# State-space products and head splits moved from GpSimd to VectorE, and small matmuls reordered, in a two-layer hybrid encoder

## The reference

```python
def mixer_ab(xn, w_in, w_out, ...):
    q, k, v, u = split(xn @ w_in)            # 1024 columns each
    o_a = dilated_attention(q, k, v, t5)     # 8 heads of 128
    y = (s5_direction(u, ..., reverse=False) + s5_direction(u, ..., reverse=True) + d_skip * u)
    y = gelu(y)
    o_b = y * sigmoid(y @ w_glu)
    return concat([o_a, o_b]) @ w_out
```

## Time and profile before

| what | us |
|---|---|
| median of 3 runs (2376.09 to 2386.47) | 2384.89 |
| the profiled execution | 2384.85 |
| its span (first to last instruction) | 2383.1 |
| busy PE, DVE, ACT, POOL | 2261.5, 1634.6, 1036.7, 285.2 |

### The profile page before, as it was taken

One profiled execution on the slowest core, in us unless ns is written; L12 is line 12 of the kernel. 1 busy time (PEld: TensorE's weight loads), 2 busy tenths in 40 slices (PEclk: granted clock), 3 DMA queues, 4 the chain that ended last, 5 costly groups with the idle time before them and its releaser, 6 DMA issues.

```text
span 2383.1 us, 40168 instructions
## 1 busy us (share of the span) xinstructions
PE 2261.5 (95%) x13779; PEld 1965.2 (82%) x13779; DVE 1634.6 (69%) x2617; ACT 1036.7 (44%) x1457; POOL 285.2 (12%) x201
## 2 busy tenths in 40 slices
PE   6887696999999999999999999999999999999997
PEld 5776576888888888888888888888888888888886
DVE  7999638767656656656658777766765765765765
ACT  6542124454444444444445444445444444444442
POOL 3560013230000000000131000022000000000023
PEclk9999798999999999999999999999999999999999
DMA  7533543556755755755755665655565566565663
GB/s 199 159 117 123 116 136 111 157 161 199 196 186 186 204 180 185 209 185 177 209 185 162 188 188 173 189 174 163 190 201 185 185 194 185 191 194 180 197 189 115
DMA packets 439240, 418.47 MB, mean 176 GB/s; under 512 B 49664, under 2 KB 434896, under 8 KB 438640
## 3 DMA queue, kind: packets, MB, share of 16 engines
q1 hardware_dynamic: 435952, 414.30, 57.6%
q10 hardware_dynamic: 3200, 3.03, 0.4%
HBM read 406.87 MB, written 10.39 MB: 175 GB/s over the span
## 4 chain that ended last, share of the span: by engine, by line
PE 84%; DVE 12%; ACT 1%; issue 1%; DMA 1%; POOL 0%; SPq 0%; DVEq 0%; ACTq 0%
PE psum L1505 53%; PE psum L1506 27%; DVE whl L916 5%; DVE ysum L916 3%; DVE wv L916 1%; PE psum L1691 1%; PE psum L1672 1%; PE psum L1669 1%; DVE wst L916 1%; DMA raw<-in_mlp_w 0%; ACT whl L599 0%; DVE tmpd L916 0%; DMA xin<-in_x 0%; PE psum L1711 0%; DVE ss_a L1237 0%
## 5 line engine op out<-in xcount | busy, mean ns | idle before, releaser
L916 DVE TENSOR_TENSOR whl<-raw,whl 128x1024 fp32r<-128x1024 f32 x744 | 964.7, 1309 | 503.3 <-ACT whl L599 501.4
L599 ACT ACTIVATE whl<-raw 128x1024 fp32r<-128x1024 f32 x744 | 788.2, 1061 | 854.7 <-PE psum L1506 740.1
L1505 PE MATMUL psum<-act,whl 128*128 128x512 f32 x3072 | 1096.5, 401 | 43.8 <-DVE whl L916 32.7
L1506 PE MATMUL psum<-act,whl 128*128 128x256 f32 x3072 | 863.1, 281 | 0.0
L1505 PEld LDWEIGHTS psum<-act,whl 128*128 128x128 f32 x3072 | 583.8, 190 | 187.7 <-DVE whl L916 33.3
L1505 PE MATMUL psum<-hid,whl 128*128 128x512 f32 x2048 | 717.3, 396 | 1.1 <-DVE whl L916 1.1
L1506 PEld LDWEIGHTS psum<-act,whl 128*128 128x128 f32 x3072 | 585.8, 191 | 0.1
L1506 PE MATMUL psum<-hid,whl 128*128 128x256 f32 x2048 | 571.3, 279 | 0.0
L1505 PEld LDWEIGHTS psum<-hid,whl 128*128 128x128 f32 x2048 | 384.4, 188 | 93.9 <-DVE whl L916 1.4
L1506 PEld LDWEIGHTS psum<-hid,whl 128*128 128x128 f32 x2048 | 385.7, 188 | 0.0
L610 ACT ACTIVATE half<-psum 128x256 f32<-128x256 f32 x376 | 123.8, 381 | 345.6 <-PE psum L1506 344.8
(11 more groups left out here) (195 smaller groups left out, 1529.4 us busy)
## 6 DMA issues: line engine op xcount, KB each, us to landing
raw<-in_mlp_w SPq DMA_DIRECT2D x512, 512.0 KB, 4.0
raw<-in_c_w_qkv SPq DMA_DIRECT2D x96, 512.0 KB, 4.6
raw<-in_ab_w_in SPq DMA_DIRECT2D x64, 512.0 KB, 4.1
raw<-in_ab_w_out SPq DMA_DIRECT2D x32, 512.0 KB, 4.3
raw<-in_c_w_out SPq DMA_DIRECT2D x32, 512.0 KB, 4.4
raw<-in_s_w_glu SPq DMA_DIRECT2D x8, 512.0 KB, 3.9
bias_c<-rpb_pad SPq DMA_DIRECT2D x64, 64.0 KB, 2.4
rpb_pad<-rpbw SPq DMA_DIRECT2D x4, 889.0 KB, 10.6
```

Of the source, the lines that this page charges most:

```text
L599: nc.scalar.activation(whl[:, s, :, 0, :], raw[:, s], ACT.Copy).then_inc(hi_done, 1)
L916: return nc.vector.tensor_tensor(dst, s0, s1, op)
L1505: pe.matmul(bank, *big, start=first, stop=False, skip_group_check=True)
L1506: last = pe.matmul(bank[:, 0:T], *little, start=False, stop=final, skip_group_check=True)
```

## The change

- **GpSimd to VectorE.** `in_weights(q, part)` makes both parts on VectorE, one quarter per block in blocks 1 to 4. `out_weights(k)` makes `fa` on VectorE: the four large operations one per sub in block 5, the eight small ones in the first three subs of block 6. `head_low` is VectorE's too. GpSimd keeps norms, masks of the second attention and small tables.
- **Ring and slots.** Transposes of quarter q stand at block q+2, the products one block later, so quarters 1 and 3 move. Scans start one sub later (25 slots for 26), `local_kernel` one block earlier.
- **Joined products.** In the first projection a pair becomes three matmuls of 256 columns into the same half bank (`joined=True`). ScalarE then copies the finished tile to its place (`take_tiles`), and VectorE's sums of blocks 0 to 15 are gone. ScalarE also takes x back (`take_x` before).
- **Mask and count.** The one-hot matrix gets a 33rd row with the logarithm of the count, or -1e30 at 0. `exps` now gives the sum (`accum_out`), VectorE only the reciprocal, and ScalarE scales (`scale_probs`).
- **Quadrants.** `chunk_outputs` puts both `mloc` products of a pair first and then steps through the quadrants.

```diff
-SCAN_SLOTS = [(j, s) for j in range(6, 13) for s in range(4)][2:]
+SCAN_SLOTS = [(j, s) for j in range(6, 13) for s in range(4)][3:]
...
@@ vector @@
+            def in_weights(q, part):
...
+                w, g0 = wst[:, q % 2, part], QG * q
+                tt(w, bcast_j(bt, 0, g0), bcast_c(aw, part, g0), ALU.mult).then_inc(w_mul, 1)
+                tt(tmpd[:], bcast_j(bt, 1, g0), bcast_c(aw, 1 - part, g0), ALU.mult).then_inc(w_mul, 1)
+                v.wait_ge(w_mul, 2 * (m + 1))
+                tt(w, w, tmpd[:], ALU.add if part else ALU.subtract).then_inc(w_done, 1)
+
+            def out_weights(k):
...
+                    made = tt(fa[:, 0], bcast_j(ct, 0, 0, NG), bcast_c(af, 0, 0, NG), ALU.mult)
+                if k == 1:
+                    v.wait_ge(ring_tr, RING["W", NQ - 1, 3] + 1)
+                    made = tt(fa[:, 1], bcast_j(ct, 1, 0, NG), bcast_c(af, 1, 0, NG), ALU.mult)
+                if k == 2:
+                    made = tt(fa[:, 0], fa[:, 0], fa[:, 1], ALU.add)
+                if k == 3:
+                    made = tt(fa[:, 1], bcast_j(ct, 0, 0, NG), bcast_c(af, 1, 0, NG), ALU.mult)
+                if k >= 4:
+                    g0 = QG * ((k - 4) // 2)
+                    here = fa[:, 1, g0:g0 + QG]
+                    if k % 2 == 0:
+                        made = tt(tmpf[:], bcast_j(ct, 1, g0), bcast_c(af, 0, g0), ALU.mult)
+                    else:
+                        made = tt(here, here, tmpf[:], ALU.subtract)
+                made.then_inc(fa_step, 1)
...
-                if j == 1 and s in (0, 2):
-                    in_weights_real(s // 2)
-                if j == 3 and s in (0, 2):
-                    in_weights_real(2 + s // 2)
+                if 1 <= j <= 4 and s in (0, 2):
+                    in_weights(j - 1, s // 2)
+                if j == 5:
+                    out_weights(s)
+                if j == 6 and s < 3:
+                    for k in ((4, 5, 6), (7, 8, 9), (10, 11))[s]:
+                        out_weights(k)
...
                 if g + 1 < HA:
-                    probs(g + 1, (g + 1) % 2, ss_a, cnt_a)
+                    inverse_sums(g + 1, (g + 1) % 2)
+                if g + 2 < HA:
+                    head_low(g + 2)
                 if g == 3:
                     for t in range(NT):
                         gelu_low(t)
@@ scalar @@
+                for n in range(2):
+                    src = psum[:, 2 * (j % 2) + n, 0:T]
...
+                    nc.scalar.activation(dst, src, ACT.Copy).then_inc(tiles_out, 1)
...
+            def scale_probs(h):
+                a.wait_ge(inv_done, h + 1)
+                for qt in range(2):
+                    nc.scalar.activation(ss_a[:, h % 2, qt], ss_a[:, h % 2, qt], ACT.Copy,
+                                         scale=stat[:, h % 2, 2, qt:qt + 1]).then_inc(prob_done, 1)
...
                 if g + 1 < HA:
-                    exps(g + 1, (g + 1) % 2, ss_a, False)
+                    exps(g + 1, (g + 1) % 2, ss_a, True)
@@ tensor @@
+                        if joined:
...
+                                parts = ((w, tile[:, 0, :]), (w, tile[:, 1, :]), little)
+                            for c, (w, m) in enumerate(parts):
+                                last = pe.matmul(bank[:, 0:T], w, m, start=(first and c == 0), stop=(final and c == 2),
+                                                 skip_group_check=True)
...
+                    for i in range(2):
+                        for g in range(2):
+                            pe.matmul(psum[NST * g:NST * (g + 1), fwd, NC * pp + 1:NC * (pp + 1)],
+                                      fa[0:NST, i, 2 * p + g].rearrange("p j c -> p (j c)"),
...
```

More of the change, by code:

```diff
@@ L540, in head_low @@
-            def head_low(h):
-                pool.wait_ge(head_hi, 2 * h + 2)
-                tt(qk_s[:, h % 3, :, 1], qk_a[:, :, h], qk_s[:, h % 3, :, 0].bitcast(F32), ALU.subtract) \
-                    .then_inc(head_split, 1)
-                tt(v_s[:, h % 3, 1].rearrange("p (k d) -> p k d", k=2), v_a[:, :, h * HD:(h + 1) * HD],
-                   v_s[:, h % 3, 0].rearrange("p (k d) -> p k d", k=2).bitcast(F32), ALU.subtract) \
-                    .then_inc(head_split, 1)
-            for h in range(HA):
-                head_low(h)
-                pool.wait_ge(mask_in, 32)
-                pool.wait_ge(bias_in[h % 2], 32 * (h // 2 + 1))
-                nc.gpsimd.tensor_tensor(bias_a[:, h % 2], bias_a[:, h % 2], neg_a[:], ALU.add).then_inc(bias_masked, 1)
@@ L853, in _ @@
                                      u[:, f].rearrange("p (j i) -> p j i", j=LC), ACT.Copy, scale=0.25).then_inc(ob_hi, 1)
-            loop_blocks(J_OUT0, 8)
+            high(0, J_OUT0, 0, 3)
+            for s in range(4):
+                for g in (2 * s, 2 * s + 1):
+                    a.wait_ge(x_tr, g + 1)
+                    nc.scalar.activation(x[:, 2 * g:2 * g + 2].rearrange("p k t -> p (k t)"), psum[:, 4 + g % 4, :],
+                                         ACT.Copy).then_inc(x_ready, 2)
+                if s < 3:
+                    high(0, J_OUT0, 1, s)
+            take_halves(0, J_OUT0, 0)
+            block_step(0, J_OUT0, 1)
+            loop_blocks(J_OUT0, 8, first=True)
             mlp(1, J_MLP0, 32)
@@ L1334, in _ @@
                     .then_inc(ob_ready, 1)
-            evac_out0 = residual(16)
-            low(0, J_OUT0, 0, 3)
-            for s in range(4):
-                take_x(2 * s)
-                take_x(2 * s + 1)
-                if s < 3:
-                    low(0, J_OUT0, 1, s)
-            evac_out0(0, J_OUT0, 0)
-            block_step(0, J_OUT0, 1, evac_out0)
-            loop_blocks(J_OUT0, 8, evac_out0, first=True)
+            loop_blocks(J_OUT0, 8, residual(16))
             def mlp(n, j0, gains, x0, h0, last=False):
@@ L1480, in norm, with sub_mm @@
                 pe.matmul(psum[:, 7, 0:T], ones[:], ssum[:], start=True, stop=True).then_inc(norm_mm, 1)
[L1482 removed]
+            def sub_mm(i, j0, jb, s, operand, ready, token_major=False, joined=False):
                 banks = 2 * ((j0 + jb) % 2)
@@ L1675, in chunk_outputs @@
                                       skip_group_check=True)
-                        for i in range(2):
-                            last = pe.matmul(psum[rows, bwd, NC * pp:NC * (pp + 1) - 1],
+                            last = pe.matmul(psum[NST * g:NST * (g + 1), bwd, NC * pp:NC * (pp + 1) - 1],
                                              fa[NST:P, i, 2 * p + g].rearrange("p j c -> p (j c)"),
@@ L1748, in v_sub @@
             def v_sub(k):
-                sub_mm(0, J_HEADS + k // 4, 0, k % 4, from_act, nothing, token_major=True)
+                sub_mm(0, J_HEADS + k // 4, 0, k % 4, from_act, nothing, token_major=True, joined=True)
             v_sub(0)
@@ L1883, in shape_constants @@
 def shape_constants():
-    rel = np.arange(T)[None, :] - np.arange(T)[:, None]
     branches = ((128, 1), (512, 4), (2048, 16))
-    cnt = sum(((rel % d == 0) & (np.abs(rel) <= w // 2)).astype(np.float32) for w, d in branches)
+    rel = np.arange(512) - 255
+    cnt = sum(((rel % d == 0) & (np.abs(rel) <= w // 2)).astype(np.float64) for w, d in branches)
+    reach = np.where(cnt > 0, np.log(np.maximum(cnt, 1)), NEG)
     c = np.arange(GRID_W)
```

266 lines of the change are left out of this document (105 added, 161 removed).

## The result

The changed kernel takes **2340.01 us** (median of 4 runs, 2338.89 to 2353.34), the kernel before beside it 2384.44 (4 runs, 2376.09 to 2386.47): ratio 0.983, 95% interval 0.981 to 0.986. The prediction, 2341, stands. The profiled execution took 2338.89, its span 2337.1 us against 2383.1 before, 46.0 less.

What follows compares the result with a forecast made beforehand. VectorE, slowed beside GpSimd and then full with scans, bounds up to 277.54 us, TensorE the rounds, then relays in the heads. From 2384.85, minus 24.0, minus 21.8, plus 1.8 gives 2341 us; range 2328 to 2364.

Steps and rivals of the forecast that it cites:

- TensorE bounds blocks 2 to 6: Before the first round: TensorE sets the pace from block 2 at 53.60 until sub (5, 0) is done at 102.9.
- VectorE then without a break: After sub (5, 0): VectorE bounds again, scans begin at 140, the first round at about 253.7.
- Stretch A: Everything up to the first round, 277.75 us before; forecast to give 24 us, bounds 16 and 30.
- Long rows are GpSimd's doing: Early VectorE work: its operations are slow where GpSimd works on long rows; one of 1.21 us takes about 3.
- rival 5: Early VectorE rows are long for another reason, such as DMA traffic, and stay; kernel slower, 2396 us; chance 3%.
- Column halves overlap: In the rounds, products of both column halves run side by side: a pair 0.70 us, a round 5.6.
- rival 1: In the rounds the column halves take turns: a pair 1.09 us, a round 8.7, total 2355; chance 15%.
- B: The stretch of rounds and subs, 277.75 to 335.30, 57.55 us before; forecast 35.7, so 21.8 us saved.
- The heads cost 1.8: Heads, after the rounds: moving low parts to VectorE keeps the relay; net cost 1.8 us, bounds -2 and +6.
- +3.2 for the detour: Heads, cycle 3: VectorE's GELU low parts stand behind `head_low(5)`, so `glu_sub` on TensorE waits 3.2 us more.
- +0.5 over the last cycles: Last cycles of the heads: reads of the accumulated sums add 0.5 us.
- C: The stretch of the heads, after the rounds; forecast to cost 1.8 us, bounds -2 and +6.

Runs made afterwards that it cites:

- pool_products: The changed kernel with the imaginary input weights and all products on `fa` back on GpSimd as before; 2359.35 us.
- unjoined: The changed kernel with the projection's products as before: two matmuls a tile, halves copied and summed; four executions took 2330.78, 2331.05, 2342.56 and 2355.12 us.
- after_again: The changed kernel itself executed once more, unedited, as a control on the same chip and in the same call; 2338.92 us.
- pool_noise: The changed kernel with twelve unneeded multiplications of 128x1024 elements on a scratch tile added on GpSimd; 2342.79 us.
- warm: The changed kernel with ninety unused matmuls of 256 columns added in TensorE's wait ahead of the first round; median 2335.88 us.
- heads_pool: The changed kernel with `head_low` back on GpSimd, all else as changed; 2339.11 us.
- quad_alone: The kernel before with only `chunk_outputs` issuing its products in the new order, both column halves side by side; 2363.44 us beside 2384.79.

## Why the prediction was right, step by step

- **TensorE bounds blocks 2 to 6.** Right. Sub (5, 0) was forecast to end at 102.9, and ends at 103.5; the low part behind it was forecast at 103.9, and starts at 104.86.
- **VectorE then without a break.** Right: scans at 141.00 (140 forecast), first round at 254.19 (253.7). Stretch A gives 23.6 us, 24 forecast. `pool_products` puts 19.0 of it on GpSimd's products and `unjoined` 3.3 on the tile sums, less what joining costs TensorE.
- **Long rows are GpSimd's doing** (against rival 5). Right and shown, by work that shares no data with VectorE's. What I put down as rows that "stretch" is a turn for each of GpSimd's instructions.
- **Column halves overlap** (against rival 1). Right and shown, in two kernels. A round takes 5.24 us and not 5.6: I had taken 0.70 for a pair, with 0.06 for dispatch that is hardly there (0.65). Subs 10.1 us (10.3), round 0 8.38 (8.6). B saves 23.3 and not 21.8. Part of that is the draw: `after_again` takes 34.1 us for B, `pool_noise` 35.4 with the same rounds, as the lower clock lasts longer behind round 0. The Trainium skill, page "TensorE: Matmul & The Clock Gate", section "Part 3: Packing small matmuls — row/col tiling", lets a weight load overlap only with another row group; by that B would have saved some 8 us. The trace does not agree: four starts within 0.02 us at 266.82, and 23.3 us. The same section's table of measured speed-ups does point this way: it has three column tiles 2.38 times faster.
- **The store at 7 us does not bound the rounds.** Right: they follow every 8.3 us.
- **The heads cost 1.8.** They cost -0.2. The terms up to `glu_sub` hold: -5.2 was forecast for moving the low parts off GpSimd (1.1 a cycle for three cycles, and 1.9 of stretched rows), and the experiments give -4.9 to -5.1; +3.2 for the detour, and they give 3.1 to 4.0, while TensorE's wait shrinks by 4.6; `glu_sub` is 1.1 later relative to the end of the rounds (0.7 forecast, with 0.9 a cycle for scalings and sums). The term that failed is the last one, "+0.5 over the last cycles". From the scores behind `glu_sub` to the output blocks the changed kernel takes 29.9 us, 1.3 less than before, and so do all its variants but `warm` (30.5) and `heads_pool`; `quad_alone`, whose heads are those of before, takes 30.7. I had priced only the accumulator's reads there. The move of the low parts is not what makes it shorter, as `heads_pool` does without it and takes 28.6; which of the other edits does was not tried. The rest is the draw: in `after_again` 1.5 us more pass between `glu_sub` and these scores, and C takes 93.6 us, 1.3 more than before.
- **The time behind the output blocks stays.** Off by 1.0 us, and no run shows why. It is 1955.2 to 1957.8 us in all profiled executions with one MLP stretch at each pace (last section), 1955.5 before and 1956.5 after.
- **Joined products cost 0.008 us a pair.** Right: 0.07 us a sub, 0.009 a pair. It is inside A's 23.6.

A gave 0.4 less than forecast, B 1.5 more and C 2.0 more, 3.1 us in all; that the total is within 1 us owes something to the 1.0 given back behind them, and to the median lying 1.1 above the profiled execution. Of the ten executions of the changed kernel seven took 2338.9 to 2341.1 us, two 2325 to 2326 and one 2353: the forecast names the most frequent time, and a single execution could have missed it by 14 us.

## What to carry to other kernels

An operation moved from GpSimd to VectorE costs VectorE its own length but frees up to one turn for every GpSimd instruction beside it (1.69 us at 128x1024); count the turns, not the rows. Where small products leave part of the array idle, put those of other rows and columns next to each other in the order before anything else. An operation that waits for a relay should not stand ahead of ready ones on its engine; one swap of that kind moved the output blocks by 2.3 us, a filler of ninety matmuls by 1.0 (3.6 and 2.3 beside the second execution of the changed kernel).

## What the hardware showed that was not expected

**TensorE has two paces at full granted clock.** Stretches of the changed kernel, then of the same kernel once more (`after_again`):

```profile
700.00:1000.00 300.00, 300.00 (x1700) 260.24 (x1699) 188.45 (x291) 127.18 (x159) 0.00 (x0) 1.00 0.64 192
2000.00:2300.00 300.00, 300.00 (x1733) 264.52 (x1731) 195.14 (x296) 129.63 (x162) 24.88 (x22) 1.00 0.61 189
```

```profile
700.00:1000.00 300.00, 300.00 (x1733) 264.49 (x1732) 191.31 (x295) 129.39 (x162) 0.00 (x0) 1.00 0.65 197
2000.00:2300.00 300.00, 300.00 (x1733) 264.54 (x1732) 191.09 (x287) 127.42 (x160) 29.91 (x27) 1.00 0.58 183
```

Identical code, TensorE never idle, clock 1.00 in all four rows, and 1700 matmuls in 300 us or 1733: a pair in 0.353 or 0.346 us. The kernel has two MLP stretches (some 500 to 1200 and 1600 to 2320 us), and a whole one keeps one pace, which makes 13 to 14 us over its length. That is nearly all of what parts the two executions, whose output blocks start within 1.3 us of each other and which end at 2337.1 and 2323.2. `unjoined` had the slower pace in both stretches (1700 and 1701) and 2353.3; before and the changed kernel have the same pair of paces (1701 and 1733, 1700 and 1733), so the pace has no part in their difference of 46.0 us. What chooses the pace stays open: it changes between executions of one kernel, and no run here tried to set it. It is also why four executions can't tell 5 us in this kernel, and a trace can.

**How long the lower clock lasts after a wait differs between executions of one kernel.** TensorE behind its wait of 8.21 us for `glu_sub`, the changed kernel (`glu_sub` starts at 343.74), then `after_again` (343.58):

```profile
346.75 0.28 PE L1721 MATMUL psum<-act,whl 128*128 128x256 f32 x1
...
350.69 0.87 PE L1668 MATMUL psum<-qk_s 128*128 128x256 f32 x6
```

```profile
349.82 0.28 PE L1721 MATMUL psum<-act,whl 128*128 128x256 f32 x1
...
352.01 0.88 PE L1668 MATMUL psum<-qk_s 128*128 128x256 f32 x6
```

The first row of each is the first of its kind at the full clock; until then such a row lasts 0.41 us. The lower clock (1.2 GHz) lasts 3.0 us in one execution and 6.2 in the other, the granted clock up to the scores is 0.79 and 0.64, and the way to them is 1.5 us longer. From the first round to the second pass 12.2 us (`after_again`) to 13.55 (`pool_noise`) for the same reason. A filler can buy such a stretch back, as `warm` shows, but the next wait of 8 us brings the lower clock again, for longer or shorter; differences of 1.5 us between two traces are no gain yet.
